# Attention outputs formed as head pairs in two column groups, from weights divided by their sums

## What is computed

```python
logits = jnp.einsum('bqhd,bkhd->bhqk', qb, kb).astype(jnp.float32) * scale
logits = jnp.where(mask, logits, -jnp.inf)
p = jax.nn.softmax(logits, axis=-1).astype(v.dtype)
outs.append(jnp.einsum('bhqk,bkhd->bqhd', p, vb))
```

## Time and profile before

| | |
|---|---|
| median of 3 runs | 1470.82 us (1469.55 to 1470.92) |
| the profiled execution's own time | 1469.74 us |
| its span in the trace | 1467.9 us |
| PE busy | 1453.4 us, 99% of the span |
| DVE busy | 931.8 us, 63% |
| ACT busy | 801.2 us, 55% |
| POOL busy | 83.0 us, 6% |
| records of PE | 7538 |

### The profile page before, as it was taken

The page is one execution under the profiler, slowest core; times in us unless marked ns, Lnnn a source line. Parts: engine busy times, 40 slices in busy tenths (PEclk is TensorE's granted clock), DMA queues, the critical chain, the costliest instruction groups (busy, mean ns, idle before and its releaser), DMA issues.

```text
span 1467.9 us, 19466 instructions
## 1 busy us (share of the span) xinstructions
PE 1453.4 (99%) x7538; PEld 1245.8 (85%) x7538; DVE 931.8 (63%) x1293; ACT 801.2 (55%) x1293; POOL 83.0 (6%) x86
## 2 busy tenths in 40 slices
PE   9999999999999999999999999999999999999998
PEld 8888888888888888888888988888888998888886
DVE  5698765565557887655555777655555678755554
ACT  6764454444467644544445786554445687644443
POOL 0112100000002220000000000000000000000000
PEclk9999999999999999999999999999999999999999
DMA  8643456666375445576564443566554444466561
GB/s 289 221 145 114 142 159 199 202 186 187 103 233 166 136 129 159 154 221 196 184 191 135 127 144 115 168 203 205 187 186 127 141 137 140 148 200 187 187 188 55
DMA packets 178699, 245.85 MB, mean 167 GB/s; under 512 B 18976, under 2 KB 130096, under 8 KB 178608
## 3 DMA queue, kind: packets, MB, share of 16 engines
q1 hardware_dynamic: 178416, 244.54, 53.5%
q10 hardware_dynamic: 192, 0.08, 0.0%
HBM read 243.52 MB, written 1.05 MB: 167 GB/s over the span
## 4 chain that ended last, share of the span: by engine, by line
PE 95%; ACT 3%; DVE 1%; issue 1%; DVEq 0%; ACTq 0%
PE acc L552 18%; PE acc L555 18%; PE acc L558 18%; PE misc L552 10%; PE misc L558 10%; PE misc L555 10%; PE misc L651 3%; PE misc L768 2%; PE misc L690 1%; PE misc L896 1%; ACT w_hi L985 1%; PE misc L714 1%; PE misc L659 1%; PE misc L836 1%; DVE w_lo L1378 1%
## 5 line engine op out<-in xcount | busy, mean ns | idle before, releaser
L1378 DVE TENSOR_TENSOR w_lo<-w_raw,w_hi 128x1024 fp32r<-128x1024 f32 (+3 forms) x472 | 558.2, 1197 | 307.0 <-ACT w_hi L985 305.6
L985 ACT ACTIVATE w_hi<-w_raw 128x1024 fp32r<-128x1024 f32 (+3 forms) x472 | 479.2, 1029 | 288.6 <-PE misc L558 164.1
L552 PE MATMUL acc<-w_hi,h_hi 128*128 128x512 f32 (+3 forms) x832 | 208.3, 373 | 3.2 <-ACT h_hi L1024 2.1
L555 PE MATMUL acc<-w_lo,h_hi 128*128 128x512 f32 (+3 forms) x832 | 201.0, 364 | 0.2 <-DVE w_lo L1378 0.2
L558 PE MATMUL acc<-w_hi,h_lo 128*128 128x512 f32 (+3 forms) x832 | 200.7, 364 | 0.0
L552 PE MATMUL misc<-w_hi,h_hi 128*128 128x512 f32 x640 | 175.5, 396 | 0.0
L555 PE MATMUL misc<-w_lo,h_hi 128*128 128x512 f32 x640 | 171.5, 390 | 0.0
L558 PE MATMUL misc<-w_hi,h_lo 128*128 128x512 f32 x640 | 171.5, 390 | 0.0
L555 PEld LDWEIGHTS acc<-w_lo,h_hi 128*128 128x128 f32 x832 | 147.8, 188 | 22.7 <-DVE w_lo L1378 0.7
L558 PEld LDWEIGHTS acc<-w_hi,h_lo 128*128 128x128 f32 x832 | 148.0, 188 | 21.6
L552 PEld LDWEIGHTS acc<-w_hi,h_hi 128*128 128x128 f32 x832 | 142.6, 189 | 23.2 <-ACT h_hi L1024 2.5
(11 more groups left out here) (207 smaller groups left out, 1272.4 us busy)
## 6 DMA issues: line engine op xcount, KB each, us to landing
w_raw<-in_w_in SPq DMA_DIRECT2D x92, 512.0 KB, 4.3
w_raw<-in_w_gate SPq DMA_DIRECT2D x176, 256.0 KB, 2.9
w_raw<-in_w_up SPq DMA_DIRECT2D x176, 256.0 KB, 3.1
w_raw<-in_w_down SPq DMA_DIRECT2D x88, 512.0 KB, 3.7
w_raw<-in_w_out SPq DMA_DIRECT2D x40, 512.0 KB, 3.6
w_raw<-in_w_in SPq DMA_DIRECT2D x32, 388.0 KB, 3.5
w_raw<-in_w_in SPq DMA_DIRECT2D x16, 336.0 KB, 4.2
w_raw<-in_w_proj_a SPq DMA_DIRECT2D x8, 512.0 KB, 4.2
```

Source lines behind the costliest of these rows:

```text
L552: pe.matmul(dst, st[0][:, k, t * P:(t + 1) * P], rhs, start=first, stop=False)
L555: pe.matmul(dst, st[0][:, k, t * P:(t + 1) * P], rhs, start=False, stop=False)
L985: act.activation(w_hi[:, g % RING, 0:w], w_raw[:, g % RING, 0:w], ACT.Copy)\
L1378: dve.tensor_tensor(w_lo[:, g % RING, 0:w], w_raw[:, g % RING, 0:w], w_hi[:, g % RING, 0:w].bitcast(F32), ALU.subtract)\
```

## The change

The group `O{g}` swaps its operands: 64 columns of values are stationary and 128 columns of turned weights move. Two heads go to partitions 0 to 63 and 64 to 127 of the bank, that is to two column groups of PE, issued alternately. The output is then already turned, so `attT0` and `attT1` are gone, and ACT and DVE split each group's output straight into `st_hi` and `st_lo`. As rows are no longer queries, the division can't follow the sum any more: `normal_weights` (DVE) multiplies the 128x512 weights in SBUF by the reciprocals ahead of the transposes, and `PT{g}` waits for it (`pn{g}`) where it waited for ACT's exponentials. In layers B two groups share one bank, so `O0`, `O2` and `O4` do the work of six. `pad` names keep the turns of the banks and do nothing.

```diff
-    plan += [("misc", "GX"), ("misc", "attT0"), ("misc", "attT1"), ("misc", "oH0"), ("misc", "oH1")]
+    plan += [("misc", "GX"), ("misc", "pad0"), ("misc", "pad1"), ("misc", "oH0"), ("misc", "oH1")]
...
-        xd1 xd1 PT0 PT1 S2 S3 xT0 xd1 O0 O1 xd1 xd2 PT2 PT3 S4 S5 xd2 O2 O3 xT1 xd2 xT2 xd2 PT4 PT5 xd3 O4 O5
-        xd3 attT0 attT1 xT3 xd3 xd3 z0 xT4 xT5 z0 cs z0 z0 xsT0 xsT2 xsT1 xsT3 cr0 z1 cb0 cb1 cr1
+        xd1 xd1 PT0 PT1 S2 S3 xT0 xd1 O0 xd1 xd2 PT2 PT3 S4 S5 xd2 O2 xT1 xd2 xT2 xd2 PT4 PT5 xd3 O4 pad0
+        xd3 xT3 xd3 xd3 z0 xT4 xT5 z0 cs z0 z0 xsT0 xsT2 xsT1 xsT3 cr0 z1 cb0 cb1 cr1
...
+def weighed_cells(block, g):
+
+    if block == 0:
+        return (2 * g, 1, 2, 0) if g < 2 else (first_head(0, g) // 2, 1, 1, 1)
+    return (0, 1, 4, 0) if g == 0 else ((g - 2) // 2, 2, 2, 1)
...
-    {**{("mla0", i): f"nT{i}" for i in range(4)}, ("uq0", 0): "cT1", ("ukv0", 0): "cT2", ("pa0", 0): "attT1",
+    {**{("mla0", i): f"nT{i}" for i in range(4)}, ("uq0", 0): "cT1", ("ukv0", 0): "cT2", ("pa0", 0): "O5",
...
-    {("wo0", 0): "attT1", ("wo0", 2): "ssT1",
+    {("wo0", 0): "O4", ("wo0", 2): "ssT1",
...
+                    if prior.startswith("pad"):
+                        prior = [m for m, v in o.turn.items() if v == u - 8][0]
...
             def weigh(layer, g):
-
                 block = layer[0]
-                group = 1 if block == 0 else HB // HKV
-                pe.wait_ge(*AC.at(layer, f"PT{g}"))
+                per_kv = 1 if block == 0 else HB // HKV
+                groups = (g,) if block == 0 else (g, g + 1)
+                for n in groups:
+                    pe.wait_ge(*AC.at(layer, f"PT{n}"))
                 b = bank_of(layer, f"O{g}")
-                pt = PTx[block][:, g % 2, :]
-                h0 = first_head(block, g)
-                heads, nk = (range(h0, h0 + 4), 1) if g < 2 else (range(h0, h0 + 2), 2)
-                for i, hd in enumerate(heads):
-                    for k in range(nk):
-                        at = (i * nk + k) * P
-                        mm = pe.matmul(b[:, i * 64:(i + 1) * 64], pt[:, at:at + P],
-                                       va[block][:, k, hd // group, :], start=(k == 0), stop=(k == nk - 1))
+                pairs, nk = (2, 1) if g < 2 else (1, 2)
+                for j, n in enumerate(groups):
+                    for m in range(pairs):
+                        cols = slice((j * pairs + m) * P, (j * pairs + m + 1) * P)
+                        for k in range(nk):
+                            for u in range(2):
+                                i = 2 * m + u
+                                at = (i * nk + k) * P
+                                mm = pe.matmul(b[64 * u:64 * u + 64, cols],
+                                               va[block][:, k, (first_head(block, n) + i) // per_kv, :],
+                                               PTx[block][:, n % 2, at:at + P], start=(k == 0), stop=(k == nk - 1))
                 mm.then_inc(*PE.mark(f"O{g}"))
...
-                    pe.wait_ge(*AC.at(layer, f"p{i}"))
+                    pe.wait_ge(*DV_.at(layer, f"pn{i}"))
                     transposes(layer, name, [Sx[block][:, i % 2, k * P:(k + 1) * P] for k in range(4)])
                 elif kind == "O":
                     weigh(layer, i)
-                elif kind == "attT":
-                    if i == 0:
-                        pe.wait_ge(*DV_.at(layer, "O5"))
-                    transposes(layer, name, [att[block][:, t, k * P:(k + 1) * P] for k in (2 * i, 2 * i + 1)
-                                             for t in range(NT)])
...
-                    act.wait_ge(*PE.at(layer, f"O{g - 2}"))
+                    act.wait_ge(*PE.at(layer, f"O{g - 2 if layer[0] == 0 else (g - 2) // 2 * 2}"))
                 act.activation(PTx[layer[0]][:, g % 2, :], b[:, :], ACT.Copy).then_inc(*AC.mark(f"PT{g}"))
+
+            def weighed(layer, g):
+                tile, step, n, t = weighed_cells(layer[0], g)
+                b = wait_bank(layer, f"O{g}")
+                act.activation(st_hi[:, tile:tile + step * (n - 1) + 1:step, t * P:(t + 1) * P],
+                               b[:, 0:n * P].rearrange("p (k q) -> p k q", k=n), ACT.Copy).then_inc(*AC.mark(f"hi.O{g}"))
...
+                    if i >= 2:
+                        weighed(layer, i - 2)
...
-                operand(layer, "attT0")
-                operand(layer, "attT1")
...
+                weighed(layer, 0)
                 channels(0)
                 mixed(1)
                 turned_weights(layer, 2)
                 turned_weights(layer, 3)
                 softmax(layer, 4)
                 softmax(layer, 5)
+                weighed(layer, 2)
                 channels(1)
                 channels(2)
                 mixed(2)
                 turned_weights(layer, 4)
                 turned_weights(layer, 5)
-                operand(layer, "attT0")
-                operand(layer, "attT1")
+                weighed(layer, 4)
...
-            def weighed(layer, g):
+            def normal_weights(layer, g):
 
                 block = layer[0]
-                n, c = (4 if g < 2 else 2), (g % 4) * 4
+                n, keys, c = (4, P, (g % 4) * 4) if g < 2 else (2, T, (g % 4) * 4)
                 dve.wait_ge(*AC.at(layer, f"p{g}"))
                 dve.reciprocal(small[:, 176 + c:176 + c + n], small[:, 160 + c:160 + c + n]).then_inc(*DV_.mark())
-                dve.wait_ge(*PE.at(layer, f"O{g}"))
-                b = misc[ORD[block].turn[f"O{g}"] % 4]
                 dve.wait_ge(*DV_.now(layer))
-                t, h0 = int(g >= 2), first_head(block, g)
-                dst = att[block][:, t, h0 * 64:(h0 + n) * 64].rearrange("p (h d) -> p h d", h=n)
+                v = Sx[block][:, g % 2, :].rearrange("p (h k) -> p h k", h=n)
                 r = small[:, 176 + c:176 + c + n].rearrange("p (h a) -> p h a", a=1)
-                dve.tensor_tensor(dst, b[:, 0:n * 64].rearrange("p (h d) -> p h d", h=n), bc(r, [P, n, 64]), ALU.mult)\
-                    .then_inc(*DV_.mark(f"O{g}"))
+                dve.tensor_tensor(v, v, bc(r, [P, n, keys]), ALU.mult).then_inc(*DV_.mark(f"pn{g}"))
+
+            def weighed(layer, g):
+
+                tile, step, n, t = weighed_cells(layer[0], g)
+                dve.wait_ge(*AC.at(layer, f"hi.O{g}"))
+                b = misc[ORD[layer[0]].turn[f"O{g}"] % 4]
+                hi, lo = (v[:, tile:tile + step * (n - 1) + 1:step, t * P:(t + 1) * P] for v in stat["st"])
+                dve.tensor_tensor(lo, b[:, 0:n * P].rearrange("p (k q) -> p k q", k=n), hi.bitcast(F32),
+                                  ALU.subtract).then_inc(*DV_.mark(f"O{g}"))
...
+                    if 1 <= i < 6:
+                        normal_weights(layer, i)
...
-                operand(layer, "attT0")
-                operand(layer, "attT1")
-
+                    if i == 0:
+                        normal_weights(layer, 0)
...
                 row_max(layer, 0)
                 row_max(layer, 1)
+                normal_weights(layer, 0)
+                normal_weights(layer, 1)
                 row_max(layer, 2)
                 row_max(layer, 3)
+                normal_weights(layer, 2)
+                normal_weights(layer, 3)
                 weighed(layer, 0)
-                weighed(layer, 1)
                 convolve(0)
                 row_max(layer, 4)
                 row_max(layer, 5)
                 weighed(layer, 2)
-                weighed(layer, 3)
+                normal_weights(layer, 4)
+                normal_weights(layer, 5)
                 convolve(1)
                 convolve(2)
                 weighed(layer, 4)
-                weighed(layer, 5)
-                operand(layer, "attT0")
-                operand(layer, "attT1")
                 split_until(layer, ORD[1].chunk_end("xd3") + LOOK)
                 dve.wait_ge(*AC.at(layer, "xd3.t1"))
```

5 lines of the change are left out of this document (3 added, 2 removed), and 1 row of the table OPERANDS.

## The result

The changed kernel takes 1492.4 us (median, 1491.8 to 1494.1), the kernel before on the same chip 1470.9: ratio 1.015, 95% interval 1.0133 to 1.0168. It is slower by 21.5 us, and 1491.5 was predicted. The profiled execution has a span of 1491.1 us, 23.2 more than before.

What follows compares the result with a forecast made beforehand. PE was taken to bound the kernel; 2 x 10.1 us (layers A) plus 2 x 0.6 (layers B) made +21.4 on 1469.74, 1491.1, with the median 1.1 above: 1491.5 was said, range 1480 to 1498.

Steps and rivals of the forecast that it cites:

- PE bound, and every new wait counts: Whole kernel: PE is busy 99% of the span, so its own time in changed pieces and every new wait count.
- The round of DVE and ACT: Layer A's loop: DVE and ACT wait for each other; rounds of 12.2, 10.7 and 11.8 us, where PE needs 9.41.
- the hop: Layer A: DVE's `weighed` waits for ACT's copy of `O` (0.4 us), where before it waited for PE alone.
- The walk without holding: Rival, layer A: POOL doesn't hold DVE's product; 4.9 us per layer, 1482 in all; chance 0.22, including half a hold.
- POOL's hold: Layer A, from iteration 1: DVE's product behind the level is held until POOL's first multiplication ends, 1.44 us.
- The clock: Rival, layer A: PE's clock falls after `PT5`'s wait, 2 us more per layer; with `G3_1` 1497; chance 0.07.
- The sign that the prediction named for it: Profile page: a clock row with digits under 9 would show the prediction wrong.
- The column groups: Merged `O` groups: matmuls in two column groups overlap; 1.2 us in B (1.7 before), 0.8 in A (gain 0.03).
- the change of form: Merged `O` groups: 0.1 us allowed on top of the overlapped matmul time.
- Layer B: +0.6 us per layer B: `O4` starts 1.9 late, waiting for ACT, and gives back 0.5 and 0.8 with `attT`.
- `oH0`: Layer A: the `attT` transposes were hidden under the wait for ACT's copy of `GX`, so dropping them saves nothing.
- the likeliest case: Whole kernel: PE's waits as summed, 1491.5 us, own range 1486 to 1495, chance 0.55.

Runs made afterwards that it cites:

- small_pool: The changed kernel with POOL's two multiplications of each level working on one column instead of 512: 1479.8 us, ratio 1.0060.
- filled_wait: The changed kernel with 30 unused identity transposes on PE in layer A, ahead of its wait for `pn5` at `PT5`: 1489.4 us, ratio 1.0128.
- o4_later: The changed kernel with layer B's `O4`, and `xT3` behind it, one slot later in PE's order: 1490.3 us, ratio 1.0132.

## Why the prediction was right

**PE bound, and every new wait counts:** right. The new waits of a layer A sum to 1.61 + 2.17 + 0.97 + 3.85 = 8.6 us, against 9.4 for the same four; the small ones (0.8 us for banks at `S5`, `G5_0`, `G6_0`) did not come. By the starts of PE's rows, which take in up to 0.2 us more at each wait, the four places cost 1.8, 2.4, 1.2 and 3.9, together 9.2 us. The excess of 11.45 is these 9.2, plus 2.6 us of clock, less about 0.4 that PE's own groups gained (0.2 was put).

**The round of DVE and ACT:** right in its links and its size (12.03, 10.67 and 11.63 us for 12.2, 10.7 and 11.8). Taking away the hop brought layer A to 4.3 us, the hold to 4.4, and the product's place with both of its costs to 2.8. The walk without holding had said 4.9, which `small_pool` meets partly by luck.

**POOL's hold:** right, 1.33, 1.10, 0.98, 0.93 and 0.90 us (the product's 2.02 to 1.59 less 0.69) where 1.44 was put from the earlier trace rows for every round. The Trainium skill's exclusion (SBUF — State Buffer, "Who interferes with whom") agrees.

**The clock:** this is the step that failed. The sum put it at nothing; it was a rival with a chance of 0.07 and an estimate of 2 us per layer A, because no row before showed the lower level. It happened in both layers A, on top of the waits. By the starts of the rows it cost 2.6 us (`PT5` 0.91 instead of 0.49, `G6` 3.31 instead of 1.71, the first sweep behind it, four matmuls of one line, 1.63 instead of 1.00) and by `filled_wait` 2.4, since `G6` there waits a little for a bank. The Trainium skill warned of it (TensorE: Matmul & The Clock Gate, "Why this matters for your kernels": gaps between bursts of matmuls take the clock to half); by that rule the trace agrees for `PT5`, with 0.50 behind 3.85 us. Of the shorter waits some were followed by a fall and some not, `G3_1`'s 2.17 us here among the latter. The sign that the prediction named for it, a clock row with digits under 9, doesn't show it.

**The column groups:** overlap, as taken. The term was mis-sized: 1.02 us for eight instead of 1.2, and 0.59 for four instead of 0.8; the 0.1 us for the change of form shows ahead of the group (1.00 us from the last sweep's start, 0.91 before). The sentence of the Trainium skill that the prediction read against overlap (TensorE: Matmul & The Clock Gate, "The mechanism": weight loads overlap matmuls in flight only when the row group differs) doesn't hold here, read that way: the two groups share the row group, and the order of the column groups alone moved eight matmuls from 1.52 to 1.02 us.

**Layer B:** +0.05 instead of +0.6. `O4` started 1.6 us late against `S0` (34.19 - 32.57) instead of 1.9, and the merged group gave back 0.7 instead of 0.5. The mechanism (all that the groups save is lost in that wait) is what `o4_later` shows.

**`oH0`:** right. From `GX` to `oH0` lie 2.00 us now, with a wait of 0.95, and 2.01 before, with `attT` in them.

**Slips in the sum:** 10.2 less 0.2 is 10.0 and not 10.1; by the prediction's own arrivals `G3_1` waits 2.3, `G4_1` 1.0 and `PT5` 3.9 us, which would make it 9.6; the walk without holding adds up to 4.8 and not 4.9; and 1491.1 with the 1.1 us between profiled execution and median is 1492.2. None of them moves the likeliest case by more than 1 us or so.

So part of the close total is luck: 2 x 10.1 + 2 x 0.6 = 21.4 was predicted, and the rows give 2 x 11.45 + 2 x 0.05 = 23.0, one term 1.3 too small and one 0.55 too large. The medians give 21.5 only because the profiled execution before lies 1.1 us under its median and the one after 0.6 above.

## What to carry to other kernels

When an edit moves work off a bounding engine, look for the rounds that it closes: a consumer that once waited for PE alone now waited for ACT, which waited for it, and none of the new costs in a round (0.7, 1.1, 0.4 us) was more than about a tenth of the layer's loss. Work that two engines do on SBUF costs by its place, so put DVE's two-input product where GpSimd is idle, and put the new work where the engine used to wait. A wait of PE of 1.3 us or more can cost 1.2 to 2.6 us on top in the clock, and need not do so in the next execution, so price it as a range, and look at windows of 2 us, since the page's row shows nothing. Look there too before calling a difference between two traces of 1 us or so unexplained.
